# Differential attention with score pieces of up to 1024 columns and a running minimum kept by the read

## The chip, the cores and the metric

The kernel runs on one core of one Trainium2 chip. The metric is the device time of one execution in microseconds (us); below 2677.91 us is the median of three runs of the kernel before.

## What is computed

The reference is one encoder block over 2048 tokens of width 1024 plus 16 meta tokens (L = 2064 positions). Its parts are an RMS norm and an input projection, four heads of differential attention, four heads of latent attention, an output projection, and a squared-ReLU MLP. The change touches the differential attention alone. In it each head has two components, each with its own queries and keys of 64 columns:

```python
def blk(qp, q1b, q2b):
    mask = _chunk_mask(qp, kpos)
    dist = jnp.abs(qp[:, None] - kpos[None, :]).astype(f32)
    bias = jnp.where(mask[None], -slopes[:, None, None] * dist[None], NEG)
    s1 = jnp.einsum('bhqd,bhkd->bhqk', q1b, k1).astype(f32) * scale + bias
    s2 = jnp.einsum('bhqd,bhkd->bhqk', q2b, k2).astype(f32) * scale + bias
    a = jax.nn.softmax(s1, axis=-1) - lam * jax.nn.softmax(s2, axis=-1)
    return jnp.einsum('bhqk,bhkv->bhqv', a.astype(v.dtype), v)
```

The mask lets a query see only keys of its own chunk of 64 and of earlier ones, so row tile i (128 queries) needs 16 + 128 (i + 1) keys.

## The kernel before

One program holds, one after the other, the input projection, the differential attention (function `attention`, 475 to 843 us of the span), the latent attention, the output projection and the MLP. `attention` handles four heads; a head has 16 row tiles ("rows" 0 to 15) of 128 queries, and each row has two components, a and b. PSUM has eight banks of 512 f32 columns: four are score buffers (`da_ps_s`, NSB = 4, lines 1132 and 1133), three hold transposes (`da_ps_t`) and one holds the output (`da_ps_o`).

The steps of a head, by their names in the code:

- **chunk** (DVE, lines 1422 to 1451; TensorE, `scores`, lines 1505 to 1521). `row_chunks` (line 1010) cuts the 144 to 2064 key columns of a component into equal pieces of at most 512 columns: 44 pieces for each component, 88 for a head. For a piece TensorE runs two matmuls into one score buffer (queries and keys are split into a high and a low part that share the contraction), after it has waited until the read of the piece four before is done (`scores_read`, line 1517). DVE then adds the bias to the scores, writes the sum to a row in SBUF and takes the maximum of the piece (`tensor_tensor_reduce`, line 1441); each such read is two instructions in the trace, the read (CUSTOM_DVE_ANT_0) and an accumulator read. After the last piece of a component DVE waits for its own accumulator and one more pair of instructions (`tensor_scalar`, line 1448) turns the piece maxima into the negated, scaled row maximum.
- **exp** (ScalarE, line 1396): the exponential over the whole row of one component, with the row sum.
- **scale** (DVE reciprocal, line 1473, then POOL, line 1388): component a of the row is divided by its sum.
- **end** (DVE, lines 1480 to 1486): a reciprocal and a one-column multiply for component b, then one pass over the whole row, a plus b times minus lambda over the sum. It waits for exp of b and for POOL.
- **turn** (TensorE line 1533, ScalarE line 1409): transposes of a key tile of four finished rows into PSUM, and the copy out. A group g is rows 4g to 4g + 3; its first turn waits for the end of row 4g + 3 (line 1525).
- **product** (TensorE line 1547): the transposed probabilities times the values, f32.

The order is one list, `STEPS`, made once by `head_steps` (line 1207) and followed by every engine, which picks its own kinds of step from it and runs them strictly in that order. `row_steps` (line 1171) places exp, scale and end a number of chunk steps after the piece that they need: exp 1, scale `SCALE_AFTER` = 2, end `END_AFTER` = 5. Whatever is still pending from a row is put behind the last piece of component a of the next row. `head_steps` then spreads turns and products over the row steps by their `cost` (line 1201: a piece costs its columns + 60, an end its columns + 250). A head has three phases (line 1252): rows 0 to 7 with the turns of group 3 of the head before, rows 8 to 11 with groups 0 and 1, rows 12 to 15 with group 2. In the first head the first phase has no turns or products; after the fourth head the turns and products of its group 3 stand alone.

`latent_attention` (line 1600) is built alike and also calls `row_chunks` (line 1647), with pieces of at most 512 columns.

## Time and profile before

| | |
|---|---|
| median of three runs | 2677.91 us (2673.85 to 2678.14) |
| the profiled execution | 2674.89 us, its span 2673.1 us |
| mean granted TensorE clock | 0.99 |
| TensorE (PE) busy over the span | 2577.9 us, 96% |
| VectorE (DVE) busy | 1628.1 us, 61% |
| ScalarE (ACT) busy | 1212.8 us, 45% |
| GpSimd (POOL) busy | 327.1 us, 12% |
| scores of differential attention on TensorE | 704 matmuls, L1519 |
| their reads on DVE | 352, L1441 |

The times come from one execution on the chip. PE is a matmul on TensorE, PEld the loading of its weights, which overlaps PE; L1519 is line 1519 of the kernel. Matmuls are pipelined: the duration shown for one runs from its start to the end of its drain, so busy time of PE counts overlaps and waits in part, and the distance from start to start says more about its rate. Busy times are sums of executed instructions; idle time is given with the instruction that released the engine. A wait for several semaphores is put down to the one that came last.

### The profile page before, as it was taken

How to read it: one execution, taken by the hardware profiler on the slowest of the kernel's cores; microseconds unless marked ns; L12 is line 12 of the kernel's file. 1: busy time of each engine (PE TensorE's matmuls, PEld its weight loads, DVE VectorE, ACT ScalarE, POOL GpSimd, SP SyncE). 2: the span in 40 equal slices, each digit the busy share in tenths (PEclk: the TensorE clock that was granted, in tenths of full speed). 3: DMA queues.
4: the chain of work that ended last, by engine and by line, in shares of the span. 5: the costliest groups of instructions: out<-in, count | busy, mean ns of one | idle time of the engine just before them, and what ended most of it. 6: DMA issues, size and time to landing. Idle time of an engine off the chain costs nothing.

```text
span 2673.1 us, 35310 instructions
## 1 busy us (share of the span) xinstructions
PE 2577.9 (96%) x12220; PEld 2117.4 (79%) x12220; DVE 1628.1 (61%) x3488; ACT 1212.8 (45%) x2177; POOL 327.1 (12%) x303
## 2 busy tenths in 40 slices
PE   8999999899998999999998999999999999999998
PEld 7997787666676888887876888878887887878786
DVE  6213303889996766764467777767767565565665
ACT  6112312577675555654444333433335353443554
POOL 1011001222221222220100000000000001111133
PEclk9999999899999999999999999999999999999999
DMA  6323456724533011116665677656645265666787
GB/s 220 128 103 106 112 165 208 185 70 102 127 131 91 29 44 40 29 60 189 190 228 183 213 234 222 216 174 214 215 137 193 104 225 103 157 170 151 190 173 136
DMA packets 331515, 398.85 MB, mean 149 GB/s; under 512 B 23488, under 2 KB 237744, under 8 KB 323024
## 3 DMA queue, kind: packets, MB, share of 16 engines
q1 hardware_dynamic: 313776, 364.68, 43.5%
q0 software_dynamic: 17568, 31.99, 8.3%
q8 instruction: 95, 1.56, 0.3%
q14 instruction: 76, 0.62, 0.1%
HBM read 240.13 MB, written 156.48 MB: 148 GB/s over the span
## 4 chain that ended last, share of the span: by engine, by line
PE 61%; DVE 2%; ACT 2%; DMA 2%; issue 1%; SPq 1%; POOL 0%; DVEq 0%; ACTq 0%; POOLq 0%
PE ff_ps_x L3113 25%; PE ff_ps_m L3113 13%; PE ff_ps_z L3113 6%; PE ml_ps_s L2026 6%; PE ff_ps_m L1586 4%; PE ml_ps_o L2055 4%; PE ml_ps_t L2039 2%; DMA ml_v_raw<-scr_yT 1%; DVE ff_mv_lo_p L2980 1%; DMA ff_pieces<-scr_acc 0%; ACT ff_mv_hi_p L2860 0%; PE ff_ps_r L2568 0%; PE mo_ps_t L2583 0%; DMA ring<-scr_u 0%; SPq L2213 0%
## 5 line engine op out<-in xcount | busy, mean ns | idle before, releaser
L3113 PE MATMUL ff_ps_x<-ff_mv_hi_p,ff_st_hi_p 128*128 128x512 f32 x764 | 298.9, 391 | 13.1 <-DVE ff_mv_lo_p L2980 13.1
L3113 PE MATMUL ff_ps_x<-ff_mv_hi_p,ff_st_lo_p 128*128 128x512 f32 x764 | 298.5, 391 | 0.0
L3113 PE MATMUL ff_ps_x<-ff_mv_lo_p,ff_st_hi_p 128*128 128x512 f32 x764 | 298.4, 391 | 0.0
L2026 PE MATMUL ml_ps_s<-wide,ml_qs 128*128 128x416 f32 (+14 forms) x880 | 197.9, 359 | 3.0 <-PEq L137 2.7
L2975 DVE TENSOR_TENSOR ff_st_lo_p<-ff_ps_m,ff_st_hi_p 128x512 fp32r<-128x512 f32 x191 | 131.5, 688 | 105.5 <-ACT ff_st_hi_p L2850 105.5
L2817 POOL DMA_DIRECT2D scr_acc<-ff_pieces x64 | 55.6, 874 | 1037.2 <-DVE ff_pieces L2999 956.3
L3113 PEld LDWEIGHTS ff_ps_x<-ff_mv_hi_p,ff_st_hi_p 128*128 128x128 f32 x764 | 144.0, 188 | 45.2 <-issue 15.5
L2867 ACT ACTIVATE ff_u<-ff_ps_x 128x512 f32<-128x512 f32 x128 | 76.6, 599 | 216.0 <-PE ff_ps_x L3113 216.0
L3113 PEld LDWEIGHTS ff_ps_x<-ff_mv_hi_p,ff_st_lo_p 128*128 128x128 f32 x764 | 144.1, 189 | 30.2
L3113 PEld LDWEIGHTS ff_ps_x<-ff_mv_lo_p,ff_st_hi_p 128*128 128x128 f32 x764 | 144.1, 189 | 29.8
L2026 PEld LDWEIGHTS ml_ps_s<-wide,ml_qs 128*128 128x128 f32 x880 | 152.4, 193 | 18.9 <-issue 7.5
L2850 ACT ACTIVATE ff_st_hi_p<-st_raw 128x512 fp32r<-128x512 f32 x191 | 119.4, 626 | 95.2 <-PE ff_ps_z L3113 95.2
L3113 PE MATMUL ff_ps_x<-wide,ff_st_hi_p 128*128 128x512 f32 x512 | 158.8, 391 | 1.2 <-ACT ff_s L2867 1.2
L2975 DVE TENSOR_TENSOR ff_st_lo_p<-st_raw,ff_st_hi_p 128x512 fp32r<-128x512 f32 x191 | 130.9, 688 | 45.1 <-ACT ff_st_hi_p L2850 43.8
L3113 PE MATMUL ff_ps_m<-wide,ff_st_hi_p 128*128 128x512 f32 x512 | 157.6, 389 | 0.0
L2850 ACT ACTIVATE ff_st_hi_p<-ff_ps_m 128x512 fp32r<-128x512 f32 x190 | 113.5, 598 | 95.6 <-PE ff_ps_m L3113 95.6
L1941 DVE CUSTOM_DVE_ANT_0 ml_rows<-ml_ps_s,ahead_bias 128x416 f32<-128x416 f32 (+14 forms) x176 | 100.1, 569 | 73.9 <-PE ml_ps_s L2026 65.1
L1547 PE MATMUL da_ps_o<-da_pT,da_v 128*128 128x512 f32 (+3 forms) x320 | 137.2, 529 | 0.0
L1864 ACT ACTIVATE ml_pT_hi<-ml_ps_t 128x512 fp32r<-128x512 f32 (+4 forms) x176 | 90.5, 536 | 97.2 <-PE ml_ps_t L2039 97.2
L1963 DVE TENSOR_TENSOR ml_pT_lo<-ml_ps_t,ml_pT_hi 128x512 fp32r<-128x512 f32 (+4 forms) x176 | 105.0, 614 | 42.6 <-ACT ml_pT_hi L1864 42.2
L1519 PE MATMUL da_ps_s<-wide,ahead_q 128*128 128x416 f32 (+14 forms) x352 | 109.5, 424 | 10.9 <-DVE da_mx L1441 10.0
L3113 PEld LDWEIGHTS ff_ps_x<-wide,ff_st_hi_p 128*128 128x128 f32 x512 | 96.8, 189 | 21.5 <-ACT ff_s L2867 1.4
(292 smaller groups left out, 6368.2 us busy)
## 6 DMA issues: line engine op xcount, KB each, us to landing
st_raw<-in_w_ff SPq DMA_DIRECT2D x64, 512.0 KB, 6.2
scr_hid<-ff_pieces SPq DMA_DIRECT2D x128, 256.0 KB, 2.6
st_raw<-scr_hid SPq DMA_DIRECT2D x64, 512.0 KB, 5.0
ring<-in_w_ff SPq DMA_DIRECT2D x28, 1024.0 KB, 7.9
scr_t<-ring SPq DMA_DIRECT2D x24, 1024.0 KB, 6.4
ring<-scr_t SPq DMA_DIRECT2D x21, 1024.0 KB, 8.2
scr_acc<-ff_pieces POOLq DMA_DIRECT2D x64, 256.0 KB, 4.0
ring<-scr_u SPq DMA_DIRECT2D x13, 1024.0 KB, 8.8
```

What stands on the lines that cost most here:

```text
L1519: m = pe.matmul(ps_s[n % NSB][:, 0:w], qs[:, g % 2, c, P * b:P * b + P], keys[u][:, 2 * c + j, k0:k0 + w], start=j == 0, stop=j == 1)
L1547: pe.matmul(ps_o[:, c0:512], v_meta[:, :] if t == 0 else v[:, t - 1], pT[0:rows_of, n % NPT, c0:512], start=t == 0, stop=t == tiles_of(g) ...
L1586: m = pe.matmul(bank, y[a][:, k], w[b][:, cols], start=k == 0 and i == 0, stop=k == KD - 1 and i == 2, skip_group_check=True)
L1864: act.activation(pT_hi[0:rows_of, n % NPT, c0:512], ps_t[n % NTB][0:rows_of, c0:512], ACT.Copy).then_inc(hi_copied, 1)
L1941: dve.tensor_tensor_reduce(out=row(i, u)[:, k0:k0 + w], in0=ps_s[n % NSB][:, 0:w], in1=bias[:, b0:b0 + w], scale=1.0, scalar=LOWEST, op0=A ...
L1963: dve.tensor_tensor(pT_lo[0:rows_of, n % NPT, c0:512], ps_t[n % NTB][0:rows_of, c0:512], f32(pT_hi[0:rows_of, n % NPT, c0:512]), ALU.subtr ...
L2026: m = pe.matmul(ps_s[n % NSB][:, 0:w], q, k, start=j == 0, stop=j == len(pairs) - 1)
L2055: m = pe.matmul(ps_o[:, c0:512], v[0:rows_of, at_v], p, start=t == 0 and j == 0, stop=t == tiles_of(g) - 1 and j == 2)
L2850: act.activation(st_hi[kind][:, :, :], stationary(kind, n % 2), ACT.Copy).then_inc(st_hi_ready, 1)
L2867: act.activation(tile, bank[:, :], ACT.Copy).then_inc(taken, 1)
L2975: dve.tensor_tensor(st_lo[kind][:, :, :], stationary(kind, n % 2), f32(st_hi[kind][:, :, :]), ALU.subtract).then_inc(st_lo_ready, 1)
L3113: m = pe.matmul(bank[:, :], w[kind][:, k], a[kind][:, k], start=start and k == 0 and i == 0, stop=stop and k == KH - 1 and i == 2, skip_gr ...
```

## The change

Score buffers become two of 1024 columns (two banks each) instead of four of 512; `row_chunks` takes the widest piece and a grain, and differential attention calls it with 1024 and 128, latent attention with 512 and 32 as before. For each piece TensorE issues two matmuls for each bank that it fills, and the next piece but one waits for its read. The read on DVE now writes minus scale times the biased score, keeps a minimum, and starts from the minimum of the piece before (a one-column operand in SBUF); for that it waits until the piece before has been read. The operation on line 1448 and its semaphore go; exp uses the last minimum directly. END_AFTER goes from 5 to 3. The order of two statements in `end` is swapped (one of them is arithmetic of the program that builds the kernel).

```diff
--- before.py
+++ after.py
@@ -1007,12 +1007,12 @@
 UP_OUTS = 8
 
 
-def row_chunks(i):
+def row_chunks(i, widest, grain):
 
 
     width = META + P * (i + 1)
-    n = -(-width // 512)
-    step = -(-width // n // 32) * 32
+    n = -(-width // widest)
+    step = -(-width // n // grain) * grain
     return [(c, min(step, width - c)) for c in range(0, width, step)]
 
 
@@ -1122,15 +1122,13 @@
         NPT = 8
         NTB = 3
         pT = mem.sb(f"da_pT", [P, NPT, 512])
-        mx = mem.sb("da_mx", [P, 2, COMPS, 5])
-        nmax = mem.sb("da_nmax", [P, 2, COMPS])
-        nmax_all = mem.sb("da_nmax_all", [P, 5])
+        lowest = mem.sb("da_lowest", [P, 2, COMPS, 3])
         total = mem.sb("da_total", [P, 2, COMPS])
         inv = mem.sb("da_inv", [P, 2, COMPS])
         inv2 = mem.sb("da_inv2", [P, 2])
         lam = mem.sb("da_lam", [P, 4])
-        NSB = 4
-        ps_s = [mem.ps(f"da_ps_s{i}") for i in range(NSB)]
+        NSB, WIDEST = 2, 1024
+        ps_s = [mem.ps(f"da_ps_s{i}", WIDEST) for i in range(NSB)]
         ps_t = [mem.ps(f"da_ps_t{i}") for i in range(NTB)]
         ps_o = mem.ps("da_ps_o")
         start_loaded, q_loaded = ahead.start_loaded, ahead.q_loaded
@@ -1140,7 +1138,7 @@
         bias_loaded = [mem.sem(f"da_bias_loaded{u}") for u in range(2)]
         v_loaded = [mem.sem(f"da_v_loaded{g}") for g in range(NG)]
         scores_ready, scores_read = mem.sem("da_scores_ready"), mem.sem("da_scores_read")
-        max_ready, exp_ready = mem.sem("da_max_ready"), mem.sem("da_exp_ready")
+        exp_ready = mem.sem("da_exp_ready")
         inv_ready, first_scaled, probs_ready = (mem.sem(f"da_{s}") for s in ("inv_ready", "first_scaled", "probs_ready"))
         inv2_step = mem.sem("da_inv2_step")
         pT_ready, pv_done = mem.sem(f"da_pT_ready"), mem.sem("da_pv_done")
@@ -1149,8 +1147,10 @@
         o_stored = ahead.o_stored
 
 
-        chunks = [(i, c, k0, n) for i in range(NT) for c in range(COMPS) for k0, n in row_chunks(i)]
+        chunks = [(i, c, k0, n) for i in range(NT) for c in range(COMPS) for k0, n in row_chunks(i, WIDEST, P)]
         NCH = len(chunks)
+        last_chunk = {(i, c): n for n, (i, c, *_) in enumerate(chunks)}
+        nth_of = lambda n: sum(1 for m in range(n) if chunks[m][:2] == chunks[n][:2])
         tiles_of = lambda g: 1 + 4 * (g + 1)
         NKT = sum(tiles_of(g) for g in range(NG))
         kt_base = [sum(tiles_of(a) for a in range(g)) for g in range(NG)]
@@ -1250,7 +1250,7 @@
 
 
         PHASES = (((0, 1), ((1, 3),), 0.2, 7), ((2,), ((0, 0), (0, 1)), 0.15, 7), ((3,), ((0, 2),), 0.2, 7))
-        SCALE_AFTER, END_AFTER = 2, 5
+        SCALE_AFTER, END_AFTER = 2, 3
         STEPS = head_steps()
 
         def walk(h, pair, u, handlers, back=(0, 1)):
@@ -1392,8 +1392,11 @@
         @stage.scalar
         def _(act):
             def exp(h, i, c, u, **at):
-                act.wait_ge(max_ready, NT * COMPS * h + COMPS * i + c + 1)
-                act.activation(comp_row(i, c, u), comp_row(i, c, u), ACT.Exp, bias=nmax[:, i % 2, c:c + 1], scale=scale,
+                n = last_chunk[i, c]
+                nth = nth_of(n)
+
+                act.wait_ge(scores_read, NCH * h + n + 1)
+                act.activation(comp_row(i, c, u), comp_row(i, c, u), ACT.Exp, bias=lowest[:, i % 2, c, nth:nth + 1], scale=-1.0,
                                accum_out=total[:, i % 2, c:c + 1]).then_inc(exp_ready, 1)
                 if isinstance(h, int) and (h, i, c) == (0, 0, 1):
                     for j in range(2):
@@ -1434,19 +1437,17 @@
                         dve.wait_ge(pT_ready, NKT * h + kt_base[2])
                     elif g != 1 and not first_head:
                         dve.wait_ge(pT_ready, NKT * (h - 1) + (kt_base[3] if g == 0 else NKT))
-                nth = sum(1 for m in range(n) if chunks[m][:2] == (i, c))
+                nth = nth_of(n)
                 b0 = (NT - 1 - i) * P + k0
+                if nth:
+
+                    dve.wait_ge(scores_read, NCH * h + n)
 
                 hold(dve, scores_ready, NCH * h + n + 1)
                 dve.tensor_tensor_reduce(out=comp_row(i, c, u)[:, k0:k0 + w], in0=ps_s[n % NSB][:, 0:w],
-                                         in1=bias[u][:, b0:b0 + w], scale=1.0, scalar=LOWEST,
-                                         op0=ALU.add, op1=ALU.max,
-                                         accum_out=mx[:, i % 2, c, nth:nth + 1]).then_inc(scores_read, 1)
-                if k0 + w == META + P * (i + 1):
-                    dve.wait_ge(scores_read, NCH * h + n + 1)
-
-                    dve.tensor_scalar(nmax_all[:, 0:nth + 1], mx[:, i % 2, c, 0:nth + 1], -scale, None, ALU.mult, ALU.min,
-                                      accum_out=nmax[:, i % 2, c:c + 1]).then_inc(max_ready, 1)
+                                         in1=bias[u][:, b0:b0 + w], scale=-scale, scalar=lowest[:, i % 2, c, nth - 1:nth] if nth else -LOWEST,
+                                         op0=ALU.add, op1=ALU.min,
+                                         accum_out=lowest[:, i % 2, c, nth:nth + 1]).then_inc(scores_read, 1)
                 if first_head and n == 1:
                     lambda_sums()
 
@@ -1475,8 +1476,8 @@
             def end(h, i, u, **at):
                 if isinstance(h, int) and (h, i) == (0, 0):
                     minus_lambda()
+                dve.wait_ge(exp_ready, NT * COMPS * h + COMPS * (i + 1))
                 n = 2 * (NT * h + i)
-                dve.wait_ge(exp_ready, NT * COMPS * h + COMPS * (i + 1))
                 dve.reciprocal(inv[:, i % 2, 1:2], total[:, i % 2, 1:2]).then_inc(inv2_step, 1)
                 dve.wait_ge(inv2_step, n + 1)
                 dve.tensor_scalar(inv2[:, i % 2:i % 2 + 1], inv[:, i % 2, 1:2], lam[:, 3:4], None, ALU.mult).then_inc(inv2_step, 1)
@@ -1515,9 +1516,11 @@
                 if not (isinstance(h, int) and h == 0 and n < NSB):
 
                     pe.wait_ge(scores_read, NCH * h + n - NSB + 1)
-                for j in range(2):
-                    m = pe.matmul(ps_s[n % NSB][:, 0:w], qs[:, g % 2, c, P * b:P * b + P], keys[u][:, 2 * c + j, k0:k0 + w],
-                                  start=j == 0, stop=j == 1)
+                for at in range(0, w, 512):
+                    cols = slice(at, min(w, at + 512))
+                    for j in range(2):
+                        m = pe.matmul(ps_s[n % NSB][:, cols], qs[:, g % 2, c, P * b:P * b + P], keys[u][:, 2 * c + j, k0 + at:k0 + cols.stop],
+                                      start=j == 0, stop=j == 1)
                 m.then_inc(scores_ready, 1)
 
             def turn(h, g, t, u, **at):
@@ -1644,7 +1647,7 @@
         const_set = mem.sem("ml_const_set")
 
 
-        chunks = [(i, k0, n) for i in range(NT) for k0, n in row_chunks(i)]
+        chunks = [(i, k0, n) for i in range(NT) for k0, n in row_chunks(i, 512, 32)]
         NCH = len(chunks)
         tiles_of = lambda g: 1 + 4 * (g + 1)
         NKT = sum(tiles_of(g) for g in range(NG))
```

The pieces of a component before and after, by row:

| row | columns | before | after |
|---|---|---|---|
| 0 to 2 | 144, 272, 400 | 1 piece | 1 piece |
| 3 to 6 | 528, 656, 784, 912 | 2 | 1 |
| 7 to 10 | 1040, 1168, 1296, 1424 | 3 | 640+400, 640+528, 768+528, 768+656 |
| 11 to 14 | 1552, 1680, 1808, 1936 | 4 | 896+656, 896+784, 1024+784, 1024+912 |
| 15 | 2064 | 5 | 768+768+528 |

## Rows read from the trace of the kernel before

**Rows 1.** Busy time by stretch: us; PE, PEld, DVE, ACT, POOL (instructions); clock, DMA, GB/s.

```profile
475.50:553.60 78.10, 69.08 (x308) 49.74 (x308) 74.17 (x300) 52.83 (x93) 17.08 (x15) 0.89 0.56 130
553.60:641.00 87.40, 84.47 (x417) 60.49 (x417) 79.02 (x305) 63.26 (x112) 19.09 (x16) 1.00 0.45 109
641.00:728.20 87.20, 84.40 (x418) 60.47 (x417) 78.82 (x305) 63.32 (x112) 19.07 (x16) 1.00 0.45 110
728.20:815.40 87.20, 84.39 (x416) 60.48 (x417) 78.50 (x302) 63.33 (x112) 19.07 (x16) 1.00 0.33 110
815.40:845.60 30.20, 24.77 (x110) 14.68 (x108) 8.89 (x22) 12.13 (x21) 1.99 (x1) 0.99 0.28 79
```

**Rows 2.** Chain that ended last, at 1450 us: twelve 512-column score-type matmuls.

```profile
1449.74 2.72 PE ff_ps_x L3113 x12
```

**Rows 3.** Instruction groups, 550 to 810 us: count, busy us, mean ns, idle before.

```profile
L1533 PE MATMUL da_ps_t<-ident,da_rows 128*128 128x128 f32 (+1 forms) x451 | 67.2, 272 | 3.8 <-DVE da_rows L1486 3.8
...
L1486 DVE SCALAR_TENSOR_TENSOR da_rows<-da_second,da_inv,da_rows 128x1936 f32<-128x1936 f32 (+15 forms) x48 | 65.7, 1369 | 3.9 <-POOL da_rows L1388 2.4
```

**Rows 4.** Timeline, TensorE, at 815 us: start, us, instruction, count.

```profile
815.52 4.04 PE L1547 MATMUL da_ps_o<-da_pT,da_v 128*128 128x512 f32 x12
```

**Rows 5.** Waits, 550 to 810 us: us in total, times, longest.

```profile
PEld da_ps_s L1519 <- DVE da_mx L1441: 18.7, 42, 1.1
...
DVE da_rows L1441 <- PE da_ps_s L1519: 5.6, 14, 0.6
```

**Rows 6.** Timeline, the first turn of the third head.

```profile
647.69 1.04 PE L1533 MATMUL da_ps_t<-ident,da_rows 128*16 128x128 f32 x8 [1.26 <-DVE da_rows L1486]
```

**Rows 7.** Busy time by stretch, parts of the first and third head; columns as in rows 1.

```profile
475.50:501.40 25.90, 17.88 (x61) 12.62 (x62) 23.75 (x123) 13.01 (x32) 5.38 (x8) 0.72 0.60 146
...
641.00:672.00 31.00, 29.21 (x152) 20.88 (x151) 26.42 (x120) 22.05 (x49) 6.96 (x8) 1.00 0.25 70
...
697.00:728.20 31.20, 30.45 (x145) 21.70 (x143) 30.31 (x105) 22.89 (x32) 6.92 (x4) 1.00 0.41 102
```

**Rows 8.** Timeline, the last row of the second head.

```profile
640.26 0.08 DVE L1441 DVE_READ_ACCUMULATOR2_ANT da_mx<- 128x1 f32 x1
...
640.40 0.63 PE L1519 MATMUL da_ps_s<-da_keys,ahead_q 128*128 128x400 f32 x2 [0.74 <-DVE da_mx L1441]
...
641.86 0.57 DVE L1441 CUSTOM_DVE_ANT_0 da_second<-da_ps_s,da_bias 128x400 f32<-128x400 f32 x1
...
642.35 0.09 DVE L1441 DVE_READ_ACCUMULATOR2_ANT da_mx<- 128x1 f32 x1
...
642.67 2.02 ACT L1396 ACTIVATE da_second<-da_second,da_nmax 128x2064 f32<-128x2064 f32 x1 [2.64 <-DVE da_nmax_all L1448]
642.69 0.31 DVE L1441 CUSTOM_DVE_ANT_0 da_rows<-da_ps_s,ahead_bias 128x144 f32<-128x144 f32 x1
642.92 0.08 DVE L1441 DVE_READ_ACCUMULATOR2_ANT da_mx<- 128x1 f32 x1
...
644.81 0.17 DVE L1480 RECIPROCAL da_inv<-da_total 128x1 f32<-128x1 f32 x1 [1.61 <-ACT da_second L1396]
...
645.26 2.37 DVE L1486 SCALAR_TENSOR_TENSOR da_rows<-da_second,da_inv,da_rows 128x2064 f32<-128x2064 f32 x1
```

**Rows 9.** Timeline, a row end of the third head.

```profile
655.73 0.08 DVE L1441 DVE_READ_ACCUMULATOR2_ANT da_mx<- 128x1 f32 x1
655.85 0.15 DVE L1448 TENSOR_SCALAR_CACHE_REDUCE da_nmax_all<-da_mx 128x2 f32<-128x2 f32 x1
...
655.93 0.16 DVE L1473 RECIPROCAL da_inv<-da_total 128x1 f32<-128x1 f32 x1
...
656.26 0.71 POOL L1388 TENSOR_SCALAR da_rows<-da_rows,da_inv 128x528 f32<-128x528 f32 x1 [1.89 <-DVE da_inv L1473]
```

**Rows 10.** Instruction group, third head: a one-column operation with a pointer operand.

```profile
L1482 DVE TENSOR_SCALAR da_inv<-da_inv,da_lam 128x1 f32<-128x1 f32 x16 | 3.4, 214 | 0.6
```

**Rows 11.** Timeline, TensorE, at 5 us: eight 16-column transposes.

```profile
5.48 1.03 PE L416 MATMUL ni_pt<-ident,ni_xn 16*128 16x16 f32 x8 [5.48 <-DMA g_eps<-in_g_attn_pre]
```

## The prediction

> **What bounds it now.** I read busy time by stretch first. Differential attention is 475.5 to 843 us; outside it nothing that a core executes changes (latent attention calls the piece function with its old numbers), so the question is four heads, with stretches of 78.1, 87.4, 87.2 and 87.2 us, and a tail [rows 1]. In heads 2 to 4 both PE and DVE look nearly full: PE 84.4 of 87.2, DVE 78.8. PE's figure has to be rebuilt from start-to-start distances, as its durations include drains.
>
> PE work of a head. Scores: 176 matmuls over 70,656 columns. In this text rows 0 to 15 are tiles of queries and bracketed rows are the trace's. Twelve matmuls of 512 columns take 2.72 us [rows 2], 0.227 each, of which 512 columns at 2.4 GHz (clock 1.00) are 0.213, so a matmul costs 0.013 plus its columns; sum 31.9 us. Transposes: 152 in a head (451 seen in 260 us [rows 3]), 0.109 each; 16.5. Products: 12 instructions, 4608 columns, in 4.04 us less a drain of 0.16 (272 ns shown for a transpose that issues in 109) [rows 3, 4], so 0.43 for 512 columns and 32.6 a head. Together 81.0 us of 87.2: PE has about 6 us of slack, not 3. DVE has 8. The waits agree: PE's weight loads waited 18.7 us for score reads in three heads, DVE 5.6 us for scores, and the first turn of a head waited 1.26 us for the end of row 15 [rows 5, 6]. Neither engine alone is the bound; they take turns. In rows 0 to 7 DVE is loose (26.4 of 31.0), in rows 12 to 15 it is full (30.3 of 31.2) [rows 7]. The first head is different: DVE is busy 74.2 of 78.1 while PE has few turns, and the granted clock is 0.72 in its first 26 us [rows 1, 7]. So the first head is DVE-bound.
>
> **DVE's side of the change, per head.** A read of 400 columns takes 0.49 us to its accumulator read, where the next could start, one of 144 takes 0.23 [rows 8]: 0.08 plus 1.03 ns a column. Columns stay. Pieces go from 88 to 52: minus 36 x 0.08 = 2.9. The row-maximum pair: from the accumulator read at 655.73 to the next operation at 655.93 [rows 9], 0.20, 32 times, 0.24 where a read follows: minus 7.0. Added: the wait of a later piece for the one before, 20 times. The nearest row is the row-maximum operation, which starts 0.12 after the accumulator read that it waits for [rows 9]: plus 2.4. Below nothing it can't be; at most the 0.20 of the whole pair, 4.0. What stands behind the wait is only the next read. The pointer operand: a one-column operation with one takes 214 ns [rows 10], the reciprocal without 160 [rows 9], so 0 to 0.05 each; I take nothing, 1.1 at the upper end. Sum: minus 7.5 (minus 4.8 to minus 9.9).
>
> The page "VectorE: DVE Perf Modes" of the Trainium skill says under "The DRAIN you can't avoid" that a semaphore between chained DVE operations costs nothing extra, only the operation count matters. Here such a wait shows 0.12 us [rows 9], so I go by the row; by the page, the 2.4 us would be 0, the first head would gain 2.4 more and the sum below would end at minus 0.4.
>
> **Where DVE gives it back.** I wrote out the step list for the new pieces. SCALE_AFTER counts pieces, and a component of rows 3 to 6 is now one piece, so the reciprocal for POOL comes after component a of the next row, right before end. POOL starts 0.33 after it and takes 0.71 for 528 columns [rows 9]; the reciprocal and end's own small operations cover 0.08 and 0.45 of that (644.81 to the pass at 645.26 [rows 8]). Row 3 stalls 0.33 + 0.71 + 0.1 for the signal - 0.53 = 0.6; rows 2 to 6 by their widths 0.5, 0.6, 0.75, 0.85 and 0.5 (two pieces cover row 6), some 3.3 us a head that were not there (rows 0 and 1 had them). END_AFTER changes nothing: an end is pushed out behind component a of the next row either way, the same columns later. Exp starts 0.2 us sooner after a component (642.67 against its last accumulator read at 642.35, 0.32, where 0.12 would do [rows 8, 9]), which nobody on the path needs but end of row 15.
>
> **PE's side, per head.** Columns stay, matmuls go from 176 to 192, and tails become narrow: a matmul costs at least 0.109, also with 16 columns (eight in 1.03, less the last one's whole 0.27 [rows 3, 11], over seven; there with f32 data and 16 rows, the nearest row). Sixteen matmuls of 16 columns (rows 3, 8, 9, 15), twenty of 128 or 144. Scores come to 34.3, plus 2.4. On the path in heads 2 to 4, as PE has little slack.
>
> **The buffers.** Four banks as before, but two units. PE may be two pieces ahead instead of four; a piece is handed over whole. Release to PE takes 0.14 (accumulator read, then PE's start [rows 8]).
>
> First head. Rows 0 to 7 on DVE: 24.9 us to 24.4 (minus 3.8 of pairs and pieces, plus 3.3 of POOL stalls); PE, even at half clock, writes a piece in the shadow of the end before. Rows 8 to 15: 53.7 to 50.7 of pure DVE work, but there PE's work (21.4 and 28.7) now equals DVE's (21.9 and 28.8), and stepping through it costs some 2 us of mutual waiting. Gain 1.5 (0 to 4).
>
> Heads 2 to 4, one cycle. From PE's last score piece to the first turn was 7.29 (640.40 to 647.69 [rows 6, 8]): reads, exp 2.14, recip and multiply 0.45, pass 2.3. After: the fourth piece of the next head stands before the turn and its buffer is freed only after the end of row 15, so 0.2 (read) + 0.14 + 0.25 come on top, and two fewer reads with 370 fewer columns, the earlier exp and no maximum come off: 7.4. From that turn to the next last piece: PE work 83.4 less 5.2 done inside the 7.4, 78.2. In this walk, step by step with the durations above, PE runs through rows 0 to 10 with 0.3 of waits and then waits 0.7, 0.45, 0.5 and 0.9 after the long ends of rows 10, 12, 13 and 14 (2.3 to 2.9 us of DVE each), because two pieces don't bridge them: 2.9. Cycle 88.5 against 87.2; I take plus 1.2 (my rounding is 0.1 to 0.4). Three cycles: plus 3.6. Tail: the wait for the last end shrinks by 0.1.
>
> Sum: minus 1.5 plus 3.6 minus 0.1 = plus 2.0 on the profiled execution's 2674.9: 2676.9. The median of the runs lies 3.0 above that execution, so 2679.9, say 2680. A measurement of this kernel tells some 0.2%, 5.4 us, from no change; this is inside.
>
> **Rivals.** (1) DVE was what held PE, faster. For it: PE's 18.7 us of waits for reads, DVE full in rows 12 to 15. Then the 7.5 us freed on DVE let PE run at its floor: 83.4 plus the two waits at the first turn (2.1) is 85.5, minus 1.7 a cycle, 5.1 in three, and the first head gives 5: 2668. Against it: PE's floor itself rises by 2.4, and the long ends still outlast two pieces. (2) The two buffers cost more, slower. Place: score pieces of rows 8 to 15 in heads 2 to 4. If PE waits 0.65 us at ten places (each end of rows 6 to 15) and not at four, waits are 6.5 instead of 2.9, a cycle 92.1 less what DVE's spare time takes back (about 1.3), so plus 3.6 each, 10.8, and the first head gains only 0.5: 2689. It decides from where PE waits over 5 us a cycle for reads. The wide piece adds to it where the step list has a product and a turn between a release and the next scores. (3) The new waits of DVE for itself are at their upper end (0.20 + 0.05): 2.6 us more in the first head, 1 each after: plus 5, to 2685; part of the slow side.
>
> **How the numbers follow.** The forecast, a near-cancellation between 2673 and 2683: 0.41. Rival 1 and in-between gains: 0.26. Rivals 2 and 3: 0.33. The range goes from rival 1's 2668, less one, to rival 2's 2689 plus two. Faster by over 0.2% 0.26, within 0.41, slower 0.33.
>
> **What would show it.** Right: DVE group L1441 at 52 reads a head, mean near 800 ns; no L1448; DVE busy about 72 us a head; the 16-column matmuls 0.11 apart; DVE's pass waiting for POOL over 8 us in total; the first stretch near 76.5 us, the others 88 to 89. Wrong: cycles below 86 (rival 1), above 90 with PE waiting for reads at every end (rival 2), or a gap over 0.2 between accumulator read and next piece of the same row (rival 3).

## The result, and the profile after

The changed kernel takes **2694.73 us** (median of four runs, 2690.6 to 2696.01), the kernel before 2675.88 us beside it: ratio 1.0065, 95% interval 1.0052 to 1.0078. It is slower by some 17 us by the ratio; forecast were 2680 in a range of 2667 to 2691, so this lies beyond its slow end. The profiled execution took 2690.6 us, its span is 2688.8 (before 2674.89 and 2673.1); it is the fastest of the four.

All of it lies in differential attention. Busy time by stretch, the same five stretches as in [rows 1] (start to start of a head's first score matmul, then the tail); columns: us; PE, PEld, DVE, ACT, POOL; clock, DMA share, GB/s:

```profile
474.80:558.00 83.20, 70.93 (x324) 51.11 (x324) 70.34 (x169) 52.31 (x93) 17.05 (x15) 0.92 0.52 122
558.00:650.00 92.00, 87.65 (x433) 62.03 (x433) 73.86 (x169) 62.58 (x112) 19.02 (x16) 1.00 0.43 104
650.00:741.80 91.80, 87.58 (x433) 61.97 (x433) 73.66 (x169) 62.49 (x112) 19.04 (x16) 1.00 0.43 104
741.80:833.50 91.70, 87.91 (x433) 62.12 (x434) 73.76 (x168) 62.54 (x112) 19.02 (x16) 1.00 0.31 105
833.50:862.80 29.30, 24.26 (x109) 14.43 (x107) 7.81 (x13) 12.12 (x21) 1.99 (x1) 1.00 0.30 81
```

Read it against [rows 1]. The first head is 5.1 us longer, the three cycles 4.6, 4.6 and 4.5, the tail 0.9 shorter: 17.9 of attention, less 2.2 by which the rest differs from one execution to the next (the span outside attention is 2303.0 and 2300.8). The granted clock is 1.00 in every cycle, as before. DVE's busy time did fall, by 5.2, 5.2 and 4.7 us a cycle and 3.8 in the first head. But its idle time, stretch less busy, went from 8.4 to 18.1 us a cycle: DVE got less to do and more to wait for.

The waits say for what. From 550 to 810 us (a little less than three cycles in both); columns: total, times, longest. First two rows of the kernel before that [rows 5] leaves out:

```profile
DVE da_inv L1480 <- ACT da_second L1396: 5.1, 5, 1.6
...
PE da_ps_s L1519 <- DVE da_mx L1441: 3.0, 6, 0.8
```

and the kernel after:

```profile
PEld da_ps_s L1522 <- DVE da_lowest L1447: 21.5, 32, 1.5
...
DVE da_inv L1481 <- ACT da_second L1399: 18.9, 28, 1.9
...
DVE da_rows L1447 <- PE da_ps_s L1522: 12.4, 24, 1.1
PE da_ps_s L1522 <- DVE da_lowest L1447: 12.2, 19, 1.3
...
DVE da_second L1447 <- PE da_ps_s L1522: 6.7, 12, 1.3
...
DVE da_second L1447 <- DVE da_lowest L1447: 3.3, 19, 0.2
```

The first row is near the 18.7 of [rows 5]: weight loads overlap a running matmul, so their waits are a poor witness. The matmuls' own wait for reads is the one to look at, 3.0 to 12.2. DVE's wait for scores went from 5.6 [rows 5] plus a row of 1.9 to 12.4 + 6.7, and its wait for ScalarE's exp of the second component, ahead of the pass that ends a row, from 5.1 to 18.9. That last one stands in no step of the prediction.

One rebuilt figure is used below: PE's work of a head, each matmul at the start-to-start cost that the prediction takes from its rows. It is 81.0 us before and 83.4 after, so a cycle holds 6.2 us that are not work before and 8.4 after. The prediction had 88.5 less 83.4, 5.1.

### The profile page after: what moved, and what is told of

The parts are those of the page before. It is cut to its first block, busy times and chain, and to the rows that moved or that the text cites. A ratio compares the mean times of both kernels' runs of the same rounds, so it can differ in the third digit from the quotient of the medians.

```text
span 2688.8 us, 34750 instructions
## 1 busy us (share of the span) xinstructions
PE 2586.7 (96%) x12284; PEld 2120.0 (79%) x12284; DVE 1609.7 (60%) x2944; ACT 1209.6 (45%) x2177; POOL 326.4 (12%) x303
## 4 chain that ended last, share of the span: by engine, by line
PE 60%; DVE 2%; DMA 2%; ACT 2%; issue 1%; SPq 1%; POOL 0%; DVEq 0%; ACTq 0%; POOLq 0%
PE ff_ps_x L3116 25%; PE ff_ps_m L3116 13%; PE ff_ps_z L3116 6%; PE ml_ps_s L2029 6%; PE ff_ps_m L1589 4%; PE ml_ps_o L2058 4%; PE ml_ps_t L2042 2%; DMA ml_v_raw<-scr_yT 1%; DVE ff_mv_lo_p L2983 1%; DMA ff_pieces<-scr_acc 0%; ACT ff_mv_hi_p L2863 0%; PE ff_ps_r L2571 0%; PE mo_ps_t L2586 0%; DMA ring<-scr_u 0%; SPq L2216 0%
## 5 line engine op out<-in xcount | busy, mean ns | idle before, releaser
L2853 ACT ACTIVATE ff_st_hi_p<-ff_ps_m 128x512 fp32r<-128x512 f32 x190 | 113.4, 598 | 95.7 <-PE ff_ps_m L3116 95.7
L1412 ACT ACTIVATE da_pT<-da_ps_t 128x512 f32<-128x512 f32 (+4 forms) x176 | 90.2, 534 | 79.2 <-PE da_ps_t L1536 78.1
L1522 PE MATMUL da_ps_s<-wide,ahead_q 128*128 128x512 f32 (+7 forms) x384 | 101.8, 391 | 17.0 <-DVE da_lowest L1447 16.0
```

Of the source, the lines that this page charges most:

```text
L1412: act.activation(pT[0:rows_of, n % NPT, c0:512], ps_t[n % NTB][0:rows_of, c0:512], ACT.Copy).then_inc(copied, 1)
L1522: m = pe.matmul(ps_s[n % NSB][:, cols], qs[:, g % 2, c, P * b:P * b + P], keys[u][:, 2 * c + j, k0 + at:k0 + cols.stop], start=j == 0, sto ...
L2853: act.activation(st_hi[kind][:, :, :], stationary(kind, n % 2), ACT.Copy).then_inc(st_hi_ready, 1)
```

## Experiments

Each run was timed beside the kernel before on its chip (medians 2671.66 to 2673.43), so the ratio is what compares. "Cycle" is the distance between the first score matmuls of heads 2 and 3 and of heads 3 and 4, each read off the trace, so of one execution of a run. Their granted clock is 1.00 but for e1 (0.96 and 0.97), e5 and e6 (0.98 over both) and the second head of e12. In first heads it lies between 0.84 and 0.94, so these compare less well.

| kernel | first head | cycles | us | ratio [95%] |
|---|---|---|---|---|
| before | 78.1 | 87.4, 87.2 | 2675.88 | |
| the change | 83.2 | 91.9, 91.8 | 2694.73 | 1.0065 [1.0052, 1.0078] |
| e1 minimum alone | 88.4 | 97.9, 95.4 | 2708.65 | 1.0131 [1.0114, 1.0148] |
| e2 wide pieces alone | 85.9 | 92.7, 92.3 | 2697.32 | 1.0097 [1.0081, 1.0112] |
| e3 own wait last | 83.3 | 91.6, 91.4 | 2689.64 | 1.0065 [1.0051, 1.0078] |
| e4 equal parts | 82.9 | 90.6, 90.6 | 2688.17 | 1.0067 [1.0049, 1.0084] |
| e5 one turn bank | 86.5 | 102.8, 102.2 | 2737.75 | 1.0248 [1.0232, 1.0264] |
| e6 e5 and third unit | 85.4 | 101.8, 101.5 | 2728.91 | 1.0212 [1.0196, 1.0227] |
| e7 reciprocal sooner | 83.6 | 95.1, 95.4 | 2701.20 | 1.0106 [1.0091, 1.0122] |
| e8 components by turns | 77.8 | 91.6, 91.6 | 2690.94 | 1.0069 [1.0055, 1.0083] |
| e9 before, handed over in pairs | 88.0 | 95.7, 95.8 | 2706.24 | 1.0124 [1.0106, 1.0142] |
| e10 e3 and e4 | 82.4 | 90.3, 90.3 | 2685.53 | 1.0039 [1.0025, 1.0054] |
| e11 e10, exp at once | 80.9 | 88.7, 88.5 | 2679.64 | 1.0021 [1.0011, 1.0030] |
| e12 before, exp at once | 78.3 | 90.5, 88.8 | 2681.06 | 1.0033 [1.0023, 1.0044] |
| e13 short rows alone | 77.6 | 86.9, 86.7 | 2671.48 | 0.9994 [0.9985, 1.0003] |

**The two halves of the change alone.** e1 keeps the chained minimum and returns to the old pieces and banks:

```
-        NSB, WIDEST = 2, 1024
+        NSB, WIDEST = 4, 512
-        ... row_chunks(i, WIDEST, P)]
+        ... row_chunks(i, WIDEST, 32)]
-        SCALE_AFTER, END_AFTER = 2, 3
+        SCALE_AFTER, END_AFTER = 2, 5
```

> Pieces, four score buffers and END_AFTER as in the kernel before; only the running minimum is taken over (each later piece of a component starts from the minimum before it and waits for it, no row-maximum operation). There are 56 such later pieces a head instead of 20. Theory A (the wait of a read for the read before and its pointer operand cost about 0.33 us, as the changed kernel's trace shows: 0.26 from accumulator read to start, and 0.07 longer for 656 columns): DVE gets 56 x 0.33 = 18.5 us more and 7.0 less a head, and as it is nearly full, the time rises by 35 to 46 us, to about 2715. Theory B (only the two whole-piece buffers and PE's matmuls cost; the wait is worth the 0.12 that I forecast): 56 x 0.12 = 6.7 against 7.0, so no change, 2676.

e2 keeps the wide pieces and two units, and returns to the maximum per piece, the row-maximum operation and exp's wait for it:

```
-                if nth:
-                    dve.wait_ge(scores_read, NCH * h + n)
-                ... scale=-scale, scalar=lowest[...] ..., op1=ALU.min, accum_out=lowest[...]
+                ... scale=1.0, scalar=LOWEST, ..., op1=ALU.max, accum_out=mx[...]
+                if k0 + w == META + P * (i + 1):
+                    dve.wait_ge(scores_read, NCH * h + n + 1)
+                    dve.tensor_scalar(nmax_all[...], mx[...], -scale, None, ALU.mult, ALU.min, ...)
```

> The changed kernel's pieces, two buffers of 1024 and END_AFTER 3, but the maxima are taken as before: one maximum per piece, an immediate start value, no wait of a read for the read before, and the row-maximum operation at the end of a component. Theory A: DVE loses 20 x 0.33 = 6.6 and gains 32 x 0.22 = 7.0 a head, so 2695 give or take 4, all of the loss is there without the running minimum. Theory B: the wait was only 20 x 0.12 = 2.4, so DVE has 4.6 us more a head and the time rises to about 2703.

Each half alone is worse than both together. In e1 there are 88 - 32 = 56 chained reads a head, and its cycles are 10.6 and 8.3 us above before. What a chained read costs is read off the timeline of the change, row 11 of the third head (start, us, instruction):

```profile
704.48 0.08 DVE L1447 DVE_READ_ACCUMULATOR2_ANT da_lowest<- 128x1 f32 x1
704.74 0.90 DVE L1447 CUSTOM_DVE_ANT_0 da_rows<-da_ps_s,ahead_bias,da_lowest 128x656 f32<-128x656 f32 x1 [0.17 <-DVE da_lowest L1447]
705.57 0.08 DVE L1447 DVE_READ_ACCUMULATOR2_ANT da_lowest<- 128x1 f32 x1
```

and a read of the same width in e2, without chain and pointer operand:

```profile
705.64 0.08 DVE L1442 DVE_READ_ACCUMULATOR2_ANT da_mx<- 128x1 f32 x1
705.64 0.84 DVE L1442 CUSTOM_DVE_ANT_0 da_second<-da_ps_s,ahead_bias 128x656 f32<-128x656 f32 x1
706.40 0.08 DVE L1442 DVE_READ_ACCUMULATOR2_ANT da_mx<- 128x1 f32 x1
```

Without the chain the read starts together with the accumulator read before it (705.64 and 705.64); with it, 0.26 us later (0.26 is also the median over the 224 chained reads of e1; without the chain the same reads start 0.00 after, in the median). And the read itself takes 0.83 instead of 0.76 to its accumulator read, 0.07 for the pointer operand. So 0.33 us per chained read, where the row-maximum pair cost 0.20 to 0.24 [rows 9]. Twenty chained reads are 6.6 us, the 32 pairs they replace 7.0: the minimum kept by the read gains nearly nothing on DVE. e2 and the change, which differ in this alone, bear it out: cycles 92.7 and 92.3 against 91.9 and 91.8. Their ratios lie further apart than that, 1.0097 and 1.0065. In the profiled executions the rest is the first head (85.9 against 83.2) and the products behind the fourth head (29.5 against 26.3 us), both at a lower granted clock in e2: 0.84 against 0.92 and 0.89 against 1.00. From row 10 of the first head on, where the clock is 1.00 in both, e2 isn't slower (45.4 us to the next head, 45.9 in the change). What the minimum is worth in the first head is thus not shown.

In e1, 56 x 0.33 - 7.0 = 11.5 us of DVE time are added, which explains its cycles: DVE is busy for 80.4 and 80.3 us and waits for itself for 56 x 0.26 = 14.6, together 95 of 97.9 and 95.4 us. Theory A of the expectation named 35 to 46 us more; it is 37.

**The order of the two waits.** e3:

```
-                if nth:
-                    dve.wait_ge(scores_read, NCH * h + n)
                 hold(dve, scores_ready, NCH * h + n + 1)
+                if nth:
+                    dve.wait_ge(scores_read, NCH * h + n)
```

> The changed kernel with two waits swapped: DVE first waits for the scores of a piece and then for the read of the piece before, so that the second can ride on the read itself. Theory A (two waits in a row cost 0.26, one 0.12): the gap falls to about 0.12 to 0.15, 20 x 0.12 = 2.4 us less of DVE a head, most of it in rows 11 to 15 where DVE is full: 2687, between 2684 and 2691. Theory B (DVE isn't what holds the heads): the gap may fall, the time stays at 2695 within 2.

```profile
704.75 0.08 DVE L1445 DVE_READ_ACCUMULATOR2_ANT da_lowest<- 128x1 f32 x1
704.87 0.90 DVE L1445 CUSTOM_DVE_ANT_0 da_rows<-da_ps_s,ahead_bias,da_lowest 128x656 f32<-128x656 f32 x1
```

The same read now starts 0.12 us behind its accumulator read: the 0.12 that the prediction took from [rows 9] is what the wait for itself costs when it comes last, with the wait for scores behind it it cost 0.26. That is 20 x 0.14 = 2.8 us of DVE time a head, and the cycle is 0.4 shorter; the ratio, 1.0065, is that of the change. Six sevenths of what DVE gains here it then waits for something else.

**Narrow matmuls.** e4 cuts a wide piece into two equal parts, one in each bank, instead of 512 and a rest:

```
-                for at in range(0, w, 512):
-                    cols = slice(at, min(w, at + 512))
+                part = w if w <= 512 else w // 2
+                for q in range(w // part):
                     ...
-                        m = pe.matmul(ps_s[n % NSB][:, cols], ...
+                        m = pe.matmul(ps_s[n % NSB][:, 512 * q:512 * q + part], ...
```

(DVE reads the two parts as one tile of two runs of columns.)

> The changed kernel, but a piece of over 512 columns is put into its two banks in equal halves (528 as 264 + 264 instead of 512 + 16) and read as two runs. Same 192 score matmuls a head, none under 264 columns but those of row 0. Theory A (narrow tails cost PE about 0.1 for 16 columns, 2.3 us a head in all, on the path in heads 2 to 4): minus 1.5 to 2.3 a head, 2687. Theory B (PE's waits for whole pieces swallow it): no change within 2, 2695.

PE's work falls to 81.2 us, the cycle by 1.2 to 1.3, between the two expectations. The price of the tails was right: with no wait in it, a piece of 528 columns takes PE 0.66 us as 512 + 16 and 0.49 as 264 + 264. But they cost the cycle only about half of the 2.4 us; PE waits for the rest anyway. The ratio, 1.0067, doesn't show the gain, e10's does (below).

**Banks.** e5 gives the transposes one bank instead of three, to learn what that costs, e6 puts the two banks so freed into a third unit:

```
-        NTB = 3
+        NTB = 1
```

```
-        NSB, WIDEST = 2, 1024
+        NSB, WIDEST = 3, 1024
```

> Control for the next run: the changed kernel with one bank for transposes instead of three, score buffers as changed (two of 1024). Each turn then waits for the copy of the turn before. Both theories: slower than the changed kernel, by 3 to 15 us a head.

> As the run before (one transpose bank), with three score buffers of 1024 instead of two, in the banks that became free. Only the number of whole-piece buffers differs between the two. Theory A (two units are what makes PE wait 6.2 us a head for reads, 2.4 before the change): a head gets 3 to 5 us shorter than in the run before, and DVE's waits for scores fall below 3 us a head. Theory B (PE waits because DVE or ScalarE are late, and a third buffer only moves the wait to the next turn or product): under 1 us a head.

Waits from 560 to 832 us in e5:

```profile
PE da_ps_t L1536 <- ACT da_pT L1412: 23.3, 35, 1.0
...
PE da_ps_s L1522 <- DVE da_lowest L1447: 5.1, 6, 1.3
```

and in e6:

```profile
PE da_ps_t L1537 <- ACT da_pT L1412: 24.0, 36, 1.0
...
PE da_ps_s L1523 <- DVE da_lowest L1447: 3.9, 2, 2.0
```

The transposes cannot give up banks: it costs over 10 us a cycle (at a clock of 0.98). Against e5, the third unit gives 0.7 to 1.0, not 3 to 5, and DVE's waits for scores don't fall. It does take away nearly all of PE's waits for reads: the two that are left in e6 stand at the start of a head, 2.0 us each. But in e5 PE waits so long at the transposes that DVE is nearly done when the scores come (5.1 us of waits, 11.6 in the change), so e6 can't say what a third unit would be worth where the transposes keep theirs. This stays open; the eight banks don't hold it.

**The reciprocal's place.** e7 puts the reciprocal for GpSimd's scaling one piece sooner:

```
-        SCALE_AFTER, END_AFTER = 2, 3
+        SCALE_AFTER, END_AFTER = 1, 3
```

> The changed kernel with SCALE_AFTER 1 instead of 2: POOL gets component a after the first piece of b, not after component a of the next row. Theory A (the constant counts pieces, so in rows 2 to 6 the pass of end waits for POOL, which matters in the first head alone, where DVE is the bound): the first head falls from 83.2 to about 80.5, the others change by less than 0.5, 2692 for 2695. Theory B (also ScalarE's order holds the later heads): over 1 us in each.

The cycles are 3.1 and 3.6 us longer, and the first head is not shorter. A wait that was 1.4 us in the change became 18.4 (560 to 832 us), the reciprocal for the exp of the first component:

```profile
DVE da_inv L1474 <- ACT da_rows L1399: 18.4, 22, 1.5
```

DVE stands in order: a reciprocal put before the next read holds that read until ScalarE is done. It is a second sign, beside the 18.9 us above, that ScalarE is late in this kernel.

**The chain hidden.** e8 (on e1's pieces) lets the pieces of the two components of a row take turns, so that a read's predecessor in the chain is two reads back:

```
-        chunks = [(i, c, k0, n) for i in range(NT) for c in range(COMPS) for k0, n in ...]
+        chunks = [(i, c, k0, n) for i in range(NT) for k0, n in ... for c in range(COMPS)]
-                    dve.wait_ge(scores_read, NCH * h + n)
+                    dve.wait_ge(scores_read, NCH * h + n - 1)
```

and DVE waits before a row's first piece of component 1 until the row two before has ended, as its tile is free only then.

> A try at a version better than both: pieces of at most 512 and four buffers as before, the running minimum, but the pieces of the two components of a row in turns (a, b, a, b), so that the read before in the same component is done long ago and the wait costs nothing; the pointer operand stays (0.07 each, 56 a head, 3.9 us), and the row-maximum operation is gone (minus 7.0). PE's work is that of the kernel before. Theory A (wait and units are the cost of the change): DVE 3 us a head less than before, heads 1 shorter by 2 to 3, the others 0 to 1: 2670, between 2664 and 2676, where before is 2673. Rival (exp of both components now comes in one lump at the end of a row, and end waits for it): slower than before by 2 to 5 us a head, 2690.

Its cycles are 3.8 and 6.4 us below e1's, its first head 10.7, and 0.3 below the kernel before: there the chain is free and the row maxima are gone. In the later heads it is 4.2 and 4.4 above before, as the rival said. Both exps of a row now fall together at its end, and DVE waits for them (18.4 us for the reciprocal of component a from 560 to 832 us).

**Units of two.** e9 changes nothing but who waits for what in the kernel before. No instruction is wider, narrower, added or moved:

```
+        units = []  # pieces of one component, two by two
         ...
-                hold(dve, scores_ready, NCH * h + n + 1)
+                hold(dve, scores_ready, NCH * h + units[unit_of[n]][-1] + 1)
         ...
-                    pe.wait_ge(scores_read, NCH * h + n - NSB + 1)
+                a = unit_of[n] - 2
+                    pe.wait_ge(scores_read, NCH * h + units[a][-1] + 1)
```

> The kernel before with its own pieces of at most 512 columns in four banks, its maxima and its list of steps, but pieces are handed over in units of up to two of one component: VectorE waits for the unit's last piece, TensorE waits until the whole unit two before is read. Nothing is added or removed on any engine. Theory (whole units of two are what costs TensorE): its idle time ahead of scores goes from 2.4 to about 6 us a head in the heads after the first, a cycle from 87.3 to 89 to 91, the time 5 to 15 us above the kernel before. Rival (what the changed kernel loses comes from narrow matmuls, chained reads and the list of steps): cycle within 0.7 of 87.3, the time within 3 us of the kernel before.

```profile
470.40:558.40 88.00, 74.59 (x308) 53.08 (x309) 75.87 (x304) 52.90 (x93) 18.05 (x16) 0.84 0.50 116
558.40:654.10 95.70, 86.97 (x416) 60.73 (x417) 78.90 (x305) 63.72 (x112) 19.08 (x17) 1.00 0.40 100
654.10:749.90 95.80, 86.92 (x416) 60.73 (x416) 78.90 (x305) 63.61 (x112) 19.06 (x17) 1.00 0.41 100
```

These are its stretches, with the columns of the table above; its waits from 550 to 810 us:

```profile
PE da_ps_s L1526 <- DVE da_mx L1448: 23.0, 32, 1.4
DVE da_rows L1448 <- PE da_ps_s L1526: 22.6, 35, 1.3
```

DVE is as busy as before, 78.90 against 78.82 [rows 1], and PE's work is the same 81.0, but the cycles are **8.3 and 8.7 us longer** and the first head 9.9. There the granted clock is 0.84 against 0.89 [rows 1], but 6.1 of the 9.9 us lie in rows 10 to 15, where it is 1.00 in both (48.8 us against 42.7). That is beyond both expectations. PE's own waits for reads went from 3.0 to 23.0 us, DVE's for scores from 5.6 to 22.6. This is the cost of two units instead of four banks by itself, in a kernel whose DVE has all its old reads, and it is larger than any other part of the change. In the change and in e9 the loss lies in the same rows: from row 8 to the end of the third head, the first score matmuls are 4.3 us further apart in the change than before, in e9 7.7.

**Exp's place in the list.** e10 joins e3 and e4:

> The changed kernel with its wide pieces cut into two equal parts, one in each bank (TensorE's work 81.2 instead of 83.4 us a head), and the wait of VectorE for its own last read put behind the wait for scores. If the two repairs add up: cycle 91.9 less 1.2 less 0.4, so 90.2 to 90.5, first head near 82.5, ratio to the kernel before near 1.0055. Rival (both gave the same thing, time that VectorE then waits elsewhere): cycle 90.6 or above.

They add up (1.7 and 1.5 us a cycle, 0.0026 of the ratio). Between e10 and e11 one line differs:

```
-                        later.append((1, ("exp", 0, i, c)))
+                        steps.append(("exp", 0, i, c))
```

> The kernel of the run before, with the exp of a component put into the list directly behind the component's last piece, so that on ScalarE it no longer stands behind the copy of a turn. Theory (ScalarE's place in the list holds VectorE: its waits for the exp ahead of the reciprocals are 6.4 us a head): these waits fall to 2 to 4 us a head and the cycle to 88 to 89, ratio 1.001 to 1.003. Rival (the waits are slack that VectorE has anyway, as TensorE hands it scores late): waits move to the scores, cycle within 0.5 of the run before, or longer, since the turn's copies come later and the transposes' banks with them.

The cycle falls by 1.6 to 1.8 us and the first head by 1.5. In the change exp goes into the list one piece after its component. That piece is now up to twice as wide, the planner spreads turns by columns, and so more turns come to stand before the exp. In the list, 12 turns of a head stand between the last piece of a second component and its exp before, 17 in the change and 8 in e11. Row 10 of the third head in the change: its second component is read by 703.19, but ScalarE first copies transposes that it has to wait for, and the exp starts 1.16 us later, while DVE will wait for it at 705.94:

```profile
703.19 0.08 DVE L1447 DVE_READ_ACCUMULATOR2_ANT da_lowest<- 128x1 f32 x1
...
703.85 0.60 ACT L1412 ACTIVATE da_pT<-da_ps_t 128x512 f32<-128x512 f32 x1 [0.65 <-PE da_ps_t L1536]
...
704.35 1.47 ACT L1399 ACTIVATE da_second<-da_second,da_lowest 128x1424 f32<-128x1424 f32 x1
...
705.94 0.16 DVE L1481 RECIPROCAL da_inv<-da_total 128x1 f32<-128x1 f32 x1 [0.30 <-ACT da_second L1399]
```

The same row in e11:

```profile
693.90 0.08 DVE L1447 DVE_READ_ACCUMULATOR2_ANT da_lowest<- 128x1 f32 x1
...
694.02 1.49 ACT L1399 ACTIVATE da_second<-da_second,da_lowest 128x1424 f32<-128x1424 f32 x1 [0.18 <-DVE da_lowest L1447]
...
696.28 0.16 DVE L1481 RECIPROCAL da_inv<-da_total 128x1 f32<-128x1 f32 x1
```

Summed over the sixteen second components of a head (start of exp less start of the last accumulator read), the lag is 6.2 us before, 12.9 in the change and 2.4 in e11. Waits from 550 to 810 us in e11:

```profile
DVE da_rows L1487 <- POOL da_rows L1388: 8.7, 15, 0.9
...
DVE da_inv L1481 <- ACT da_second L1399: 5.9, 5, 1.9
```

ScalarE's 18.9 is down to 5.9, and GpSimd's wait has come out behind it, 8.7 us in three heads, which ScalarE's had covered in the change.

e12 makes the same edit in the kernel before:

> The kernel before with one edit: the exp of a component stands in the list directly behind its last piece, where the last run of the changed kernel gained 6 us by it. Theory (that gain was the repair of something the change brought, since before VectorE waited only 1.9 us a head for the exp against 6.4 after): cycle within 0.5 of 87.3, the time within 3 us of the kernel before. Rival (the place is bad for any version): cycle 85.6 to 86.4, about 5 us faster than before, a version that beats both.

Neither came true: it is 0.0033 slower. In the third head all of it is in row 3 (1.67 us more, every other row within 0.03). In the second head row 3 is 3.3 us longer; the granted clock is 0.78 there. Waits from 550 to 810 us:

```profile
PE da_ps_o L1547 <- ACT da_pT L1409: 6.6, 3, 2.2
```

Three times PE waits 2.2 us for a copy behind which a product stands: ScalarE now does the exp first. So no place of the exp is good in itself. It fits a list or it doesn't, and the old place fitted the old pieces.

**DVE's time alone.** e13 drops the row-maximum pair in rows 0 to 2 of the kernel before, where a component is one piece and the read's own minimum is the row's. No chain, no units, same list.

```
-     ... scale=1.0, scalar=LOWEST, op1=ALU.max, accum_out=mx[...]
-                if k0 + w == META + P * (i + 1):
+     ... scale=-scale if single(i) else 1.0, ..., accum_out=nmax[...] if single(i) else mx[...]
+                if not single(i) and k0 + w == META + P * (i + 1):
```

> The kernel before with its pieces, its four banks and its list of steps. Only in rows 0 to 2, where a component is a single piece, the read is scaled by -scale and keeps the minimum itself, so that six row-maximum pairs of 0.20 to 0.24 us a head are gone with nothing put in their place. Theory (VectorE is the bound of the first head and takes turns with TensorE later): first head shorter by 1.0 to 1.4 us, the later cycles by 0 to 0.6, the time 1 to 3 us below the kernel before, about the smallest difference that can be told. Rival (in rows 0 to 2 the ends and GpSimd's pass are waited for, VectorE's time there is free): first head within 0.5 of 78.1, cycles within 0.3, the time within 1 us.

The six pairs are 1.3 us of DVE time a head; first head and cycles are shorter by 0.4 to 0.6 us each (for the first head 1.0 to 1.4 were expected). The ratio 0.9994 has 1 within its interval, so the time can't be told from the kernel before; it is the only version here that isn't slower.

## Why the prediction was wrong

The point that failed is the cycle of heads 2 to 4, "plus 1.2" each where 4.6 were measured, and the first head, "minus 1.5" where it was plus 5.1. The steps behind it are the price of two whole units ("2.9" of waits in a cycle, "some 2 us of mutual waiting" in the first head) and exp's place in the list, which was taken as free.

**What held.** PE's work: 83.4, with the 16 added matmuls. Score pieces of DVE: 52 a head. DVE's busy time is 73.7 where "about 72" was said. The turn of a head: 7.4 forecast from the last score piece to the first turn, 648.68 to 656.40 = 7.72 measured, and the place is the one named, the next head's fourth piece, which waits for the end of row 15:

```profile
656.05 0.52 PE L1522 MATMUL da_ps_s<-wide,ahead_q 128*128 128x272 f32 x2 [1.26 <-DVE da_lowest L1447]
656.40 0.60 PE L1536 MATMUL da_ps_t<-ident,da_rows 128*16 128x128 f32 x4
```

Nothing outside attention moved. The tail lost 0.9, forecast 0.1. "END_AFTER changes nothing" is right: with the new pieces, 3 and 5 give the same list, step for step.

**DVE's term, "minus 7.5".** The self-wait was taken as 0.12 and the pointer operand as nothing. They are 0.26 and 0.07, beyond the "upper end" of rival 3 (0.20 + 0.05). With the term's own 2.9 and 7.0 that makes 2.9 + 7.0 - 6.6, so minus 3.3. The step's error was the row it was read from: in [rows 9] an operation that waits for one thing, whereas a later piece waits for itself and then for scores; e3, with the order turned, gives the 0.12 back. "VectorE: DVE Perf Modes" of the Trainium skill (section "The DRAIN you can't avoid") has such a wait at no cost, measured there on copies; the traces here show 0.26 and 0.12 us and don't agree. For the time this matters little, as e3 gives only 0.4 us a cycle for 2.8 of DVE time.

**"Exp starts 0.2 us sooner ... which nobody on the path needs".** This is the wrong step whose price is most directly measured. I had the signal 0.2 us sooner (0.12 behind the accumulator read at its best, as said) and had seen that SCALE_AFTER counts pieces, but not that the exp's own delay of one piece does too. Second components' exps start 6.7 us a head later in sum, the ends wait for them, and with the delay gone the cycle is 1.7 shorter (e11 against e10, so on top of those two repairs). The "3.3 us a head" of GpSimd stalls was computed for an exp in time: the change shows 1.0 us in three heads, e11, where the exp is in time, 8.7, about what was forecast.

**The buffers, "2.9" of waits in a cycle.** From the head's first turn to its last score piece (656.40 to 740.48) the change takes 84.1 where the walk had 78.2 + 2.9 = 81.1; with the 0.3 at the turn these are the missing 3.3 us of the cycle. Exp's place is 1.7 of them and the dearer chain 0.4, as the repairs give it back; about 1.2 is left for what the walk underrated in the handover (an attribution by difference, not by a run of its own). The place is plain: PE's idle time ahead of scores, by the rebuilt figure, is 4.9 us in rows 2 to 15 of the third head, 1.3 of it in row 11, behind the end of row 10, where the walk had 0.7, and 2.0 in row 15, behind the end of row 14, where it had 0.9. Rival 2 had the side, the place (rows 8 to 15) and with "92.1" even the cycle, but then took off 1.3 for "DVE's spare time", to plus 3.6, and gave the first head a gain. Its sign, PE waiting over 5 us a cycle for reads, did show: PE's idle time ahead of scores in a whole cycle, by the rebuilt accounting, is 6.2 us (before 2.4); the profile's own row, which counts no wait that a drain covers, has 12.2 in nearly three cycles, some 4.3 each.

**The first head, "some 2 us of mutual waiting".** I called it DVE-bound, so that freed DVE time should come out of it. The change freed 3.8 us and the head is 5.1 longer: rows 0 to 7 by 1.4, where 0.5 less was forecast, and rows 8 to 15 by 3.7, where 1.0 less was forecast. e9 shows the reason: with whole units the head grows by 9.9 at equal work on each engine, 7.7 of it in rows 8 to 15. This head was DVE-bound because four banks kept scores ready; with two units it isn't any more.

**The whole account of a cycle** (means of the two), from run to run: before 87.3; whole units 95.7 (e9, +8.4); the wide pieces, with their fewer reads, narrow tails and list, 92.5 (e2, -3.2); chained minimum for row maxima 91.9 (the change, -0.7); equal parts and the wait last 90.3 (e10, -1.6); exp at once 88.6 (e11, -1.7). The prediction had small gains and losses that nearly cancelled; in this order of steps a loss of 8.4 stands against a gain of 3.9. The shares hold for this order alone: no run adds the units last, and the wide pieces bring fewer reads, narrow tails and a new list at once. That DVE's savings reach the time here because a faster reader shortens the handover fits e9, but no run shows it alone. What is left of e11 against before (+1.3 a cycle, +2.8 in the first head) is unsettled in its parts.

No version beats the kernel before by more than a measurement tells; e13 is the nearest.

## What to carry to other kernels

Fewer, larger buffers of the same total are a change of their own, and it can be tested alone: leave every instruction as it is and make the two sides wait for whole units. Where an operation's delay in a list counts pieces, wider pieces move it; after such a change look on each engine at what stands ahead of the instruction that others wait for. And price a chained instruction by a row with all the waits that it will carry, against the operation that it replaces.

## What the hardware showed that was not expected

A DVE read that waits for the one before it starts 0.26 us after that one's accumulator read if the wait for itself comes first and a second, met one follows, and 0.12 us if it comes last. The trace has a difference between the two: in the change both waits stand in a semaphore instruction of their own, 0.05 us long, between the accumulator read (704.48) and the read (704.74), and the read carries no wait; in e3 the wait for scores stands alone and was over before, and the read itself carries the wait for the one before it. A pointer operand lengthens a read of 656 columns from 0.76 to 0.83 us, and one of 512 (e1 against before, medians) from 0.61 to 0.68.
